# A hybrid decoder layer on one core: the table of distance biases stored in eight parts, and the first two weight slabs of the heads split one by one

## What is computed

```python
h = rms_norm(x, g_pre_mix)
q, k, v, iq, iw, ik, hq, hf, hi, hg, ga, gb = split(h @ w_in)
mk, mv = mem_kv(mem, g_mem, w_xk, w_xv)             # keys and values of 256 memory tokens
o_a = dsa(q, k, v, iq, iw, ik, rel_bias)            # top-k indexer, gathered attention, distance bias
o_b = hgrn2(hq, hf, hi)                             # gated linear recurrence, 16 heads
u = sigmoid(ga) * o_a + sigmoid(gb) * rms_norm(o_b) * silu(hg)
x = x + rms_norm(u @ w_out)
x = x + rms_norm(cross_attend(x, mk, mv))
x = x + rms_norm(conv_ffn(x))
```

## Time and profile before

| | |
|---|---|
| median of 3 runs | 2966.31 us (2964.43 to 2966.59) |
| the profiled execution | 2961.16 us, of which 2959.6 us are the profile's span |
| PE busy | 2809.9 us (95%) |
| PEld, DVE, ACT, POOL busy | 2655.8, 1666.5, 1069.6, 211.5 us |
| mean granted TensorE clock | 0.969 of full speed |
| moved by DMA | 460.24 MB, 156 GB/s |

### The profile page before, as it was taken

One profiled execution on the slowest core, in us unless ns is written; L12 is line 12 of the kernel. 1 busy time (PEld: TensorE's weight loads), 2 busy tenths in 40 slices (PEclk: granted clock), 3 DMA queues, 4 the chain that ended last, 5 costly groups with the idle time before them and its releaser, 6 DMA issues.

```text
span 2959.6 us, 46627 instructions
## 1 busy us (share of the span) xinstructions
PE 2809.9 (95%) x18716; PEld 2655.8 (90%) x18716; DVE 1666.5 (56%) x2355; ACT 1069.6 (36%) x1323; POOL 211.5 (7%) x303
## 2 busy tenths in 40 slices
PE   8899999999999999999989987989999999989995
PEld 7889887799999999999979865979999999989994
DVE  5464563287777878787453322365555555553344
ACT  4233444343434444444342332333232323332332
POOL 0102211010111111110000000000000000000002
PEclk9999999999999999999999997989999999999998
DMA  9756645654545545555454565535555555435553
GB/s 284 146 147 183 201 157 165 213 157 130 158 130 157 143 136 150 136 151 142 127 166 128 185 224 197 152 121 148 150 148 150 148 149 149 131 110 154 146 151 101
DMA packets 692708, 460.24 MB, mean 156 GB/s; under 512 B 13454, under 2 KB 661230, under 8 KB 686318
## 3 DMA queue, kind: packets, MB, share of 16 engines
q1 hardware_dynamic: 679952, 414.25, 49.0%
q0 software_dynamic: 8960, 30.47, 3.9%
q10 hardware_dynamic: 3712, 14.35, 1.3%
HBM read 429.91 MB, written 29.13 MB: 155 GB/s over the span
## 4 chain that ended last, share of the span: by engine, by line
PE 91%; DVE 3%; DMA 2%; ACT 2%; issue 1%; POOL 1%; POOLq 0%; SPq 0%; ACTq 0%; DVEq 0%
PE psum L577 19%; PE psum L583 19%; PE psum L574 19%; PE psum L813 4%; PE psum L1155 3%; PE psum L1156 3%; PE psum L1157 3%; PE psum L966 2%; PE psum L818 2%; PE psum L944 1%; PE psum L1057 1%; DMA ring<-in_w_in 1%; PE psum L947 1%; PE psum L940 1%; DMA h<-in_cache_mem_v 1%; PE psum L677 1%
## 5 line engine op out<-in xcount | busy, mean ns | idle before, releaser
L1196 DVE TENSOR_TENSOR w_low<-ring,w_high 128x2048 fp32r<-128x2048 f32 x292 | 675.4, 2314 | 395.2 <-ACT w_high L1826 394.8
L1826 ACT ACTIVATE w_high<-ring 128x2048 fp32r<-128x2048 f32 x294 | 561.5, 1911 | 781.5 <-PE psum L583 589.6
L574 PE MATMUL psum<-x_high,w_high 128*128 128x320 f32 x3808 | 609.3, 312 | 2.9 <-ACT w_high L1826 2.9
L577 PE MATMUL psum<-x_high,w_low 128*128 128x320 f32 x3808 | 601.5, 310 | 8.5 <-DVE w_low L1196 8.5
L577 PEld LDWEIGHTS psum<-x_high,w_low 128*128 128x128 f32 x3808 | 571.8, 189 | 9.1 <-DVE w_low L1196 9.0
L574 PEld LDWEIGHTS psum<-x_high,w_high 128*128 128x128 f32 x3808 | 568.7, 188 | 10.6 <-issue 3.5
L583 PE MATMUL psum<-h_low,w_high 128*128 128x320 f32 x3360 | 528.1, 309 | 0.0
L583 PEld LDWEIGHTS psum<-h_low,w_high 128*128 128x128 f32 x3360 | 502.8, 188 | 0.0
L1155 PE MATMUL psum<-y_high,w_down_high 128*128 128x320 f32 x704 | 219.9, 312 | 15.7 <-DVE w_low L1758 15.7
L1156 PE MATMUL psum<-y_low,w_down_high 128*128 128x320 f32 x704 | 218.1, 310 | 0.0
L1157 PE MATMUL psum<-y_high,w_low 128*128 128x320 f32 x704 | 218.1, 310 | 0.0
(11 more groups left out here) (391 smaller groups left out, 3088.6 us busy)
## 6 DMA issues: line engine op xcount, KB each, us to landing
ring<-in_w_in SPq DMA_DIRECT2D x128, 1024.0 KB, 5.6
ring<-in_w_up SPq DMA_DIRECT2D x88, 1024.0 KB, 5.6
ring<-in_w_down SPq DMA_DIRECT2D x64, 704.0 KB, 4.7
ring<-in_w_xk SPq DMA_DIRECT2D x16, 1024.0 KB, 5.5
ring<-in_w_xv SPq DMA_DIRECT2D x16, 1024.0 KB, 5.0
ring<-in_w_out SPq DMA_DIRECT2D x16, 1024.0 KB, 5.8
ring<-in_w_xq SPq DMA_DIRECT2D x16, 1024.0 KB, 5.9
ring<-in_w_xo SPq DMA_DIRECT2D x16, 1024.0 KB, 6.1
```

What stands on the lines that cost most here:

```text
L574: mm(out, w_hi[:, j % 2, k, :], x_hi[:, k, :], start=k == 0, stop=False)
L577: mm(out, w_lo[:, j, k, :], x_hi[:, k, :], start=False, stop=False)
L1196: V.tensor_tensor(w_lo[:, j], ring[:, j], w_hi[:, j % 2].bitcast(FP32), ALU.subtract).then_inc(N.slab_lo, 1)
L1826: F(w_hi[:, j % 2], ring[:, j], ACT.Copy).then_inc(N.slab_hi, 1)
```

## The change

The store of the bias table becomes eight DMAs of two heads each (392 KB). POOL issues part g once `slab_used` has reached 12 + g, that is behind tiles 11 to 18, and its copy `ik_dup` now comes ahead of them. The reader waits for all eight.

At the heads, ACT copies slab 64 once tile 62 has ended and slab 65 once tile 63 has ended, each ahead of the `memory_evac` of that place; DVE makes slab 64's low part ahead of the last memory evacuation. `by_chunks` waits for each tile's own `slab_hi` and no longer for those of both tiles at the start; its wait on `bank_free` is one more for a stage with one tile and the same as before for two.

```diff
+BIAS_PARTS = 8
...
                     if q == 0:
+                        pe.wait_ge(N.slab_hi, n0 + j + 1)
                         pe.wait_ge(N.slab_lo, n0 + j + 1)
...
-                pe.wait_ge(N.bank_free, s0 + FREE + tiles - 2)
-                pe.wait_ge(N.slab_hi, n0 + tiles)
+                pe.wait_ge(N.bank_free, s0 + FREE)
...
             for n in range(29, 32):
                 slab_low(B_MEM + n, n % R)
+            slab_low(B_HG, 0)
             memory_out(31)
             dve.wait_ge(N.o_evac, H + DB)
...
-            for j in range(2):
-                slab_low(B_HG + j, j)
+            slab_low(B_HG + 1, 1)
...
             high(31)
+            act.wait_ge(N.slab_used, B_HG - 1)
+            slab_high(0, 16 * (B_HG // R + 1))
             memory_evac(30)
             input_back(2)
+            act.wait_ge(N.slab_used, B_HG)
+            slab_high(1, 16 * (B_HG // R + 1))
             memory_evac(31)
             input_back(3)
             send(31)
...
             act.wait_ge(N.o_evac, H + DB)
-            first_highs(B_HG)
             act.wait_ge(N.memo_sent, 128)
...
-            pool.wait_ge(N.setup_evac, 2)
-            pool.dma_start(bias_dram, dist_sb[0:H, :].rearrange("h (o n) -> h o n", o=1).broadcast_to([H, P, NDIST])).then_inc(N.bias_stored, 16)
             pool.wait_ge(N.ikpage_loaded, 16 * DB * NPG)
             pool.wait_ge(N.ik_mm, 1)
             G.tensor_copy(ik_dup, ...)
+            pool.wait_ge(N.setup_evac, 2)
+            for g in range(BIAS_PARTS):
+                pool.wait_ge(N.slab_used, B_V + g)
+                h = slice(g * H // BIAS_PARTS, (g + 1) * H // BIAS_PARTS)
+                pool.dma_start(bias_dram[h], dist_sb[h, :].rearrange("h (o n) -> h o n", o=1)
+                               .broadcast_to([H // BIAS_PARTS, P, NDIST])).then_inc(N.bias_stored, 16)
...
-            pool.wait_ge(N.bias_stored, 16)
+            pool.wait_ge(N.bias_stored, 16 * BIAS_PARTS)
```

## The result

| | before | changed |
|---|---|---|
| median of 6 runs each | 2965.37 us (2961.04 to 2967.43) | 2976.66 us (2971.68 to 2979.92) |
| the profiled execution, its span | 2961.16, 2959.6 us | 2971.68, 2970.1 us |
| PE busy | 2809.9 us | 2812.7 us |

A forecast was written before the change was run, and what follows sets the result against it. PE bounds the kernel, with 91% of the chain, so its stands count. Removed stall 17.8 plus first head tile 4.9 less cost of the eight stores 12.8 gives 9.9 us gained: 2956 us, range 2943 to 2977.

The forecast's parts named there:

- What bounds the kernel, part 1: PE's wait at the value-tile transposes: the bias store delays slab 14; that stall of 17.8 us goes.
- Part 2, the length of a part: Two-head bias stores: two engines each, 15.5 us plus 2.5 alone, 30.9 us for two overlapping neighbours.
- The 26: Bias stores: 26 GB/s shared by about four neighbouring rows, from two large packets at the kernel's end at 13 GB/s each.
- the forecast's own rule: Slab loads beside bias stores: need less allowance and earlier stands gives each slab's lateness, 11.0 us in sum.
- Part 2, the slabs: Loads of slabs 15 to 22: slab 15 late by 5.2 us, 16 to 18 in time, 19 to 22 by 0.8 to 2.6.
- Half clock: PE's matmuls behind the 5.2 us stand at slab 15: one spell at half clock, costing 1.8 us.
- Part 3: First head tile: stand shrinks from 5.8 to 2.6 us, half clock behind it goes; gain 4.9 us, ends 1.5 and 5.
- The fourth quarter of `x_high`: First head tile: PE may next wait for this load, which can take back up to 2 us.
- Part 4: `by_chunks` in the four later stages: looser wait worth nothing, ten more waits cost below 0.5 us.
- Sum: Whole kernel: 17.8 + 4.9 - 12.8 = 9.9 us gained, median 2956 us.
- Rival (a): Bias stores are hidden, spread over more engines or slabs keep their share: 2943.6 to 2945.6 us, chance 0.27.
- Rival (c): Bias stores last 32 us, at 6.2 GB/s an engine or successive ones on the same two: slower, 2978.6 us, chance 0.17.

The follow-up runs named there:

- run 3: Changed kernel, but each of the eight stores writes 16 of the 128 repeats of all 16 heads: 2942.23 us, ratio 0.9931 to before.
- run 6: Changed kernel, but only heads 0 and 1 in a two-head store, the other 14 heads later in eight stores of all 14: 2942.00 us.
- run 5: Changed kernel, but part g stores heads g and g + 8, rows eight partitions apart: 2942.75 us, ratio 0.9926 to before.
- run 9: Changed kernel, but only the first two two-head stores at their events, the other 12 heads later in eight stores of all 12: 2946.85 us.
- run 1: Changed kernel with the bias store back as one DMA at its old place; heads and `by_chunks` edits kept: 2960.07 us, ratio 0.9987 to before.
- run 2: Changed kernel with the eight stores kept, heads and `by_chunks` edits put back as before: 2978.22 us, ratio 1.0049 to before.
- run 4: Changed kernel, but the eight two-head stores stand behind every second tile: 2972.67 us, ratio 1.0032 to before.
- run 8: Changed kernel, but heads 0 to 7 in four two-head stores at every third tile, heads 8 to 15 in four eight-head stores behind: 2942.36 us.
- run 7: Changed kernel, but the bias table lies on all 128 partitions and is stored in one DMA at the old place: 2945.95 us, ratio 0.9931.
- run 10: Changed kernel, but two two-head stores, two events apart, the other 12 heads later in eight stores of all 12: 2945.54 us, ratio 0.9937.

## Why the prediction was wrong

**What bounds the kernel, part 1.** Right. The store was what kept slab 14 away (it lands after 5.6 us now), and all 17.8 us came back at tiles 13 to 15. In run 3, where nothing takes their place, the whole gain stands.

**Part 2, the length of a part.** Right in mechanism, and short in size by some 4 us where parts overlap. Two engines: the 12.3% of run 6 show it. That agrees with the rule of "DMA: Bandwidth & Descriptors", section "Why a DMA increments its semaphore by 16 and not by 1", of the Trainium skill. Two neighbouring rows share one path (25 GB/s in run 6 against 47 in run 5), and so do two neighbouring parts (25 GB/s in run 9); the forecast had 26. The 26 came by way of two packets of another transfer, so that it fits this well is partly luck. Alone a part took 18.8 us from issue to landing against 18.0 forecast. For the second of a pair the forecast had 25.5, 23.0 and 2.5, and run 9 has 29.4. With 3.9 more for every slab the forecast's own rule would give stands of 18.8 us instead of 11.0, an estimate. But the length alone doesn't decide: run 9 has such a pair, and 2.3 us of stands.

**Part 2, the slabs: the step that failed.** I gave every slab the same price, that of its own part: "Slab 15 then needs 2.5 + 23.0 + 2.0 = 27.5 us against 22.3", and "Slabs 16 to 22 take the same with 1 us more, because SP's issue is held while the slab ahead drains". Both halves are wrong. Slab 15 is issued just ahead of its part and is on its way before it: 6.8 us. It is slab 16, issued with part 0 under way, that takes 27.5, and that this is the forecast's very number is luck. And the hold of SP's issue is no 1 us but 14.3 and then 26.9. I had the row for it, 23.7 us in the earlier trace rows, and counted it as an effect of the stall that the change removes. A held issue moves the load to later, towards parts that POOL issues on its own event meanwhile, and it lands in their midst. I had at most two parts, four engines, under way at once; the queue shows up to almost nine, and the DMA share from 125 to 215 us, which I had said would rise, fell from 0.68 to 0.55. So the lateness is not 5.2 us once and small rests, with slabs 16 to 18 in time. It grows along the queue: 4.48 us of stand behind slab 16, 15.12 behind slab 17, 1.53 behind slab 18, whose issue was held longest. The next loads are held 15.7 and less as the parts thin out, since POOL waits for the same tiles. One more stand of 2.92 follows at 248 us, behind a load issued at 220.1 that met the part of 222.07. Stands: 24.0 for 11.0. Run 9 has the first two parts and none of those that follow, and there slabs 17 and 18 land after 24.7 and 14.2 us and PE stands 2.3.

**Half clock.** 7.1 us for 1.8. The forecast had one spell, behind a single stand of 5.2; there were three, behind the stands of 4.48, 15.12 and 2.92, and none behind that of 1.53.

**Part 3.** The stand was right (2.70 for 2.6), the price 3.9 us (1.2 to 6.5) for 4.9. The 1.8 of it that I took from the end of half clock behind the stand hardly came, because a stand of 2.70 us is followed by it too, in all profiles that have this stand but that of run 3 (the matmuls 0.27 apart above for 3.3 us; the earlier trace rows had PEclk 0.50 for 3.6). That the price still came near is in part luck, since the memory stage ahead lost some 3 us in run 1 as well and the later starts gave some back. The fourth quarter of `x_high` took nothing back.

**Part 4.** Nothing, as said: runs 2 and 1 add up to the whole change without it, within what they tell (0.49% and -0.13% against 0.39%).

**Sum and rivals.** With the measured terms the sum is 17.8 + 3.1 - 31.1, and 3.1 lost in the memory stage and 2.7 won at the later starts, by the clock, make it -10.6: the difference at the last tile. Rival (a) is what wide parts do, not these. Rival (c) gave nearly this time, 2978.6, but by another mechanism: its parts of 32 us on each engine don't occur alone (18.8), and successive parts don't sit on the same two engines, since the queue's share grows with them. Its deciding length, "a part of about 27 us", is just about reached by the second of the pair in run 9 (29.4 from issue), and there PE stands 2.3 us and the kernel is faster than before. What decides is the distance between narrow stores against the time that a held load needs: 8 us is too close and 15 to 21 us still are (run 4), 24 to 27 us are enough (run 8); or the length of each, about 6 us shorter is enough (run 5).

**A better version.** Runs 3, 5, 6 and 8 lie within 1 us of each other at 2942 us, 0.7 to 0.8% below before and, by the ratios to before, 1.1 to 1.2% below the changed kernel, with which they were not run side by side. Run 3 is the simplest: the loop stays, and only the slice goes over the repeats instead of the heads.

**Why a load gets next to nothing beside a store.** The trace of before shows it, from 131 to 147 us, where both queues are on all engines:

```profile
q0 software_dynamic: 337, 1.59, 96.2%
q1 hardware_dynamic: 336, 0.17, 3.6%
```

They take turns, one packet each, but a packet of the store has 4.7 KB and takes 0.73 us (96.2% of sixteen engines for 16 us, through 337), one of the load has 0.5 KB and takes 0.03. A slab is 128 such packets for each engine. By an estimate from these rows it would need some 97 us on an engine that a store of this pace keeps busy.

**Open.** When SP is let go: in the changed kernel that is at 154.0, 181.1 and 197.1 us, 4.5 to 5.3 us ahead of the landing of the load before, so when that load is nearly through. What it is that frees SP was not tried by itself. And of the 46 and 47 us of slabs 17 and 18 no run tells how much comes from the narrow stores that follow and how much from their piling up on six and more engines. Run 4, where they hardly overlap, has landings up to 32.1 and still 21.6 us of stands.

## To carry to other kernels

Cut a store into parts along a dimension that leaves all DMA engines in each part; a part on two engines took three times as long here (18.8 us for 6.1), and a load issued meanwhile waits for its share on these two. Where a queue issues in order, a load held at one narrow transfer can be moved to the next one: price the whole train of issues behind it, not each load beside its own neighbour. And a long issuing instruction in the profile of before (here 23.7 us of SP) is a cost of the next design as well, as long as anything narrow stays in it.

## What I had not expected of the hardware

- SP's issue of one 1024 KB load stood up to 26.9 us behind stores of two engines each, and two loads issued beside them landed 46.3 and 47.4 us later, though one narrow store of 392 KB is over after 18.8 us.
- POOL's last store issues are late too, for "issue" and for no wait that the trace shows: the eighth in the changed kernel began at 222.07 us, 11 us behind its tile's end at 211.2. In the run with heads eight apart the eighth is behind by "issue" as well, with 12.71 us idle before it. In both it begins 0.4 us after the landing of the seventh (221.7 and 190.3 us). The wide parts of run 3 go at their events throughout, and each of them has landed before the next. What holds the eighth was not tried.
- A stand of 2.70 us was followed by half clock within 1 us of the restart in the changed kernel and in runs 1 and 4 to 10, and by none in run 3. And a stage that did the same matmuls (the end of the memory stage) took 30.4 us instead of 27.1, with PEclk 0.84 for 0.96, in the changed kernel and in runs 1 and 2 alike. A difference of some 3 us between two kernels can come from that alone.
